# Layer 1's context keys and values woven into the latents' input projection, and stationary-only operands shifted by 64 bytes

## The reference, cut to what matters

```python
h = modulate(x, lp["g_norm1"], sh1, sc1)
hc = modulate(xc, lp["g_norm1"], modc[..., :d], modc[..., d:2 * d])
proj = h @ lp["w_in"]
n_in_c = IN_COLS if update_ctx else KV_COLS
projc = hc @ lp["w_in"][:, :n_in_c]
k_mla_l, v_mla_l, k_gqa_l, v_gqa_l = mixer_kv(proj[..., :KV_COLS], lp, rope_mla, rope_gqa)
k_mla_c, v_mla_c, k_gqa_c, v_gqa_c = mixer_kv(projc[..., :KV_COLS], lp, None, None)
...
def mixer_kv(kvc, lp, rope_mla, rope_gqa):
    c_kv, k_rope, k_g, v_g = jnp.split(kvc, ...)
    kv = (rms_norm(c_kv, lp["g_ckv"]) @ lp["w_ukv"]).reshape(b, l, MLA_HEADS, MLA_NOPE + MLA_V)
    ...
```

## Time and profile before

| | us |
|---|---|
| median of 3 runs | 2702.24 (2700.51 to 2708.99) |
| the profiled execution's own time | 2704.51 |
| its span in the trace | 2702.7 |
| PE busy in it | 2525.1 (93%) |
| PEld / DVE / ACT / POOL busy | 2216.8 / 1595.2 / 1326.6 / 582.2 |

### The profile page before, as it was taken

How to read it: one execution, slowest core, us unless ns; L and a number is a source line. 1 busy time by engine, 2 the same in 40 slices (tenths; PEclk the granted TensorE clock), 3 DMA queues, 4 the chain that set the end, 5 groups by cost and what they waited for, 6 DMA issues and landing times.

```text
span 2702.7 us, 46044 instructions
## 1 busy us (share of the span) xinstructions
PE 2525.1 (93%) x17246; PEld 2216.8 (82%) x17246; DVE 1595.2 (59%) x2386; ACT 1326.6 (49%) x2127; POOL 582.2 (22%) x430
## 2 busy tenths in 40 slices
PE   6999999999899996999999999997999899989997
PEld 5877898887689985875899799786898699758986
DVE  3655676567477755664777465435665544455445
ACT  3434565444547643445466445444544554455444
POOL 1111333210023322110233233020231232012311
PEclk8999999999999997999999999999999899999999
DMA  8575455546145553465556556562366466524663
GB/s 273 175 233 188 149 179 185 181 145 217 36 154 171 179 163 101 149 196 179 170 157 187 185 184 200 160 184 93 115 188 192 145 181 195 163 83 130 186 200 116
DMA packets 332944, 450.52 MB, mean 167 GB/s; under 512 B 28192, under 2 KB 207392, under 8 KB 332768
## 3 DMA queue, kind: packets, MB, share of 16 engines
q1 hardware_dynamic: 332400, 446.58, 52.8%
q0 software_dynamic: 368, 1.57, 0.2%
HBM read 446.99 MB, written 1.05 MB: 166 GB/s over the span
## 4 chain that ended last, share of the span: by engine, by line
PE 86%; DVE 7%; ACT 4%; issue 2%; DMA 1%; POOL 1%; SPq 1%; DVEq 0%; ACTq 0%; POOLq 0%
PE S L925 28%; PE S L916 23%; PE G L925 14%; PE G L916 9%; PE TB L978 2%; PE S L1007 2%; PE G L867 1%; PE G L1045 1%; ACT pp L1318 1%; DVE wlo L672 1%; ACT whi L666 1%; PE TB L891 1%; PE G L1030 1%; DVE nmx L1795 1%; PE S L1115 1%
## 5 line engine op out<-in xcount | busy, mean ns | idle before, releaser
L672 DVE TENSOR_TENSOR wlo<-raw,whi 128x1024 fp32r<-128x1024 f32 (+4 forms) x630 | 796.4, 1274 | 748.3 <-ACT whi L666 744.3
L666 ACT CAST whi<-raw 128x1024 fp32r<-128x1024 f32 (+2 forms) x776 | 771.7, 1008 | 754.0 <-PE S L916 280.8
L925 PE MATMUL S<-hhi,whi 128*128 128x256 f32 x1952 | 547.0, 280 | 4.1 <-issue 2.4
L925 PE MATMUL S<-hhi,wlo 128*128 128x256 f32 x1952 | 546.7, 280 | 0.0
L925 PE MATMUL S<-hlo,whi 128*128 128x256 f32 x1952 | 546.6, 280 | 0.0
L672 POOL TENSOR_TENSOR wlo<-raw,whi 128x1024 fp32r<-128x1024 f32 (+3 forms) x146 | 335.8, 2300 | 788.8 <-ACT whi L666 788.1
L925 PEld LDWEIGHTS S<-hhi,whi 128*128 128x128 f32 x1952 | 367.1, 188 | 5.7 <-issue 5.1
L925 PEld LDWEIGHTS S<-hlo,whi 128*128 128x128 f32 x1952 | 367.8, 188 | 0.1
L925 PEld LDWEIGHTS S<-hhi,wlo 128*128 128x128 f32 x1952 | 366.9, 188 | 0.0
L925 PE MATMUL G<-hhi,whi 128*128 128x256 f32 x1088 | 305.5, 281 | 1.9 <-issue 1.8
L925 PE MATMUL G<-hlo,whi 128*128 128x256 f32 x1088 | 304.8, 280 | 0.0
(11 more groups left out here) (336 smaller groups left out, 4227.9 us busy)
## 6 DMA issues: line engine op xcount, KB each, us to landing
raw<-in_ffn_wi SPq DMA_DIRECT2D x352, 256.0 KB, 3.5
raw<-in_w_up SPq DMA_DIRECT2D x264, 256.0 KB, 3.5
modw<-in_w_mod SPq DMA_DIRECT2D x192, 256.0 KB, 4.9
raw<-in_w_in SPq DMA_DIRECT2D x192, 256.0 KB, 3.0
raw<-in_ffn_wo SPq DMA_DIRECT2D x160, 256.0 KB, 3.5
raw<-in_w_down SPq DMA_DIRECT2D x120, 256.0 KB, 3.3
raw<-in_a_wqkv SPq DMA_DIRECT2D x72, 256.0 KB, 2.9
raw<-in_w_o SPq DMA_DIRECT2D x48, 256.0 KB, 3.3
```

Of the source, the lines that this page charges most:

```text
L666: act.copy(whi[:, n0 % SPLIT, z, w], raw[:, n0 % RAW, z, w]).then_inc(hi_done, 1)
L672: eng.tensor_tensor(wlo[:, n0 % SPLIT, z, w], raw[:, n0 % RAW, z, w], whi[:, n0 % SPLIT, z, w].bitcast(F32), ALU.subtract)\
L925: mm = pe.matmul(out_[:, m * T:(m + 1) * T], w, x, start=first and c == 0 and m == 0 and z == 0, stop=last and c == kc - 1 and z == len(te ...
```

## The change

It has two parts.

**The order in layer 1.** After the context's two `in` units the latents' `norm` comes at once. Its squares are taken by ACT after the context's first unit and its means by DVE after the second (`early`). Then the context's `prep` runs on DVE between the lo parts of the latents' first two `in` units (`part=0`), `ctrans` follows, the third unit (`part=1`), `gqat`, `ukv`, then the last two units (`part=2`) with the context's `heads` woven in, then `mlat`. The context's projected columns go to an unused place in `qkv1` (`rows_base`, `C_ASIDE`), and in these parts DVE makes every lo part (`lo_by_pool` returns False).

**Addresses.** Operands that only ever stand stationary are placed so that they start at a multiple of 128 bytes: `rhi` 125568 and `rlo` 117376 (new names over the same space as `hhi` and `hlo`, for `qkv`, `pgate` and `wo1`), `crT` 105088, `b_fhi` 174080 and 146176, `b_flo` 146176 and 168704, `b_phi` 154368. `hhi` and `hlo` of the `norm` stages and of the wide `norm2` ones, which are moving in `gates` and `up`, stay 64 past such a multiple, as do the attention outputs. To make room, the 8-column tensor `mx` is dropped and its users write to `ssq` or in place to `nmx`. The weights start at 72192 and 88576, still multiples of 128.

```diff
+SHIFT = 16
...
+            if l == DEPTH - 1:
+
+                add("prep", rq=2, rr=2, l=l, s=CTX, full=False)
+                gemm("in", 2, KD, l=l, s=s, splits=splits[:2], part=0)
+                add("ctrans", tk=1, sa=1, l=l, full=False)
+                gemm("in", 1, KD, l=l, s=s, splits=splits[2:3], part=1)
+                add("gqat", tk=1, s=CTX, full=False)
+                gemm("ukv", 2, 2, l=l, s=CTX)
+                add("heads", rq=2, rr=2, l=l, s=CTX, full=False)
+                gemm("in", 2, KD, l=l, s=s, splits=splits[3:], part=2)
+                add("mlat", tk=4, s=CTX, full=False)
...
-        sb("align_weights", [P, 24])
...
-        sb("align_operands", [P, 16])
+        sb("align_operands", [P, SHIFT])
...
+        ybuf, hlo, rlo, probT0 = region(KD * T + SHIFT, [("ybuf", 0, [P, NT, D], F32), ("hlo", 0, [P, KD, T], F32R),
+                                                         ("rlo", SHIFT, [P, KD, T], F32R), ("probT0", 0, [P, KD, T], F32)])
+        hhi, rhi, probT1 = region(KD * T + SHIFT, [("hhi", SHIFT, [P, KD, T], F32R), ("rhi", 0, [P, KD, T], F32R),
+                                                   ("probT1", 0, [P, KD, T], F32)])
...
-             ("b1_fhi", o1["gT"], [P, NF, T], F32R),
-             ("b1_flo", 0, [P, NF, T], F32R),
+             ("b1_fhi", o1["gT"] + SHIFT, [P, NF, T], F32R),
+             ("b1_flo", SHIFT, [P, NF, T], F32R),
...
+        def by_rows(st):
+            return (hhi, hlo) if st.wide else (rhi, rlo)
...
-            if st.kind in ("wo2", "gates") or st.kind == "down" and not st.conv or st.kind == "br" and st.part == 0:
+            if st.kind in ("wo2", "gates") or st.kind == "down" and not st.conv or st.part is not None and st.kind in ("br", "in") and (st.kind, st.part) != ("br", 1):
                 return False
...
+                        if k == 0 and early(st):
+                            act.wait_ge(bank_free[1], st.u + 1)
+                            for t in range(NT):
+                                row_squares(early(st), t)
...
+                    if st.part in (0, 2):
+                        work = prep_rows(before(st, "prep")) if st.part == 0 else head_rows(before(st, "heads"))
+
+                        def lo_and_rows(n0, *slot):
+                            lo_part(dve, n0, *slot)
+                            next(work, None)
```

More of the change, by code:

```diff
@@ L559, in inner, with early, rows_base @@
             return z if z and z.kind == "norm" else None
+        def early(st):
+            z = STAGES[STAGES.index(st) + 1] if st.kind == "in" else None
+            return z if z and z.kind == "norm" else None
+        def rows_base(st):
+            full = st.full if st.kind in ("prep", "ctrans", "heads") else st.s == LAT or st.l < DEPTH - 1
+            return 0 if full else C_ASIDE
         def inside(st):
@@ L1090, in _ @@
                                 tr.then_inc(turned_done, 1)
-                elif st.kind in ("in", "qkv", "pgate"):
+                elif st.kind == "in":
                     product(st, hhi, hlo, False)
+                elif st.kind in ("qkv", "pgate", "wo1"):
+                    product(st, rhi, rlo, False)
                 elif st.kind == "gates":
@@ L1096, in _ @@
                     pe.wait_ge(rows_ready, st.rr)
-                    srcs = [0, P] + ([C_CQ + c * P for c in range(Q_RANK // P)] if st.full else [])
+                    base = rows_base(st)
+                    srcs = [base, base + P] + ([C_CQ + c * P for c in range(Q_RANK // P)] if st.full else [])
                     for n in range(st.counts["tk"]):
@@ L1235, in _ @@
                 if st.kind == "norm" and not inside(st):
-                    if st.which == "1" and st is not norms[0]:
+                    if st.which == "1" and st is not norms[0] and not early(STAGES[STAGES.index(st) - 1]):
                         for t in range(NT):
@@ L1572, in prep_rows @@
                     k3 = q1[:, t, C_KG:C_VG].rearrange("p (h d) -> p h d", h=GQA_KV)
+                    if not st.full:
+                        rope_keys(st, t)
                     link(dve.tensor_copy(kdup1[:, t, :, 0], k3))
@@ L1673, in _ @@
                     if st is not norms[0]:
-                        for t in range(NT):
-                            row_mean(st, t)
+                        if not early(STAGES[STAGES.index(st) - 1]):
+                            for t in range(NT):
+                                row_mean(st, t)
                         for t in range(NT):
@@ L1717, in rows_in, with unit_and_rows @@
                         bank(st, 1, k)
-                        dve.tensor_copy(qkv1[:, 1, c0:c1], acc(st, j, 1)[:, 0:c1 - c0]).then_inc(bank_free[1], 1)
-                    units(st, rows_in)
-                elif st.kind == "prep":
-                    if not st.full:
-                        for _ in prep_rows(st):
-                            pass
+                        base = rows_base(st)
+                        dve.tensor_copy(qkv1[:, 1, base + c0:base + c1], acc(st, j, 1)[:, 0:c1 - c0]).then_inc(bank_free[1], 1)
+                        if k == 1 and early(st):
+                            for t in range(NT):
+                                row_mean(early(st), t)
+                    if st.part in (0, 2):
[3 more added lines that the diff above has]
+                            next(work, None)
+                        def unit_and_rows(k, j, i):
+                            split_weights(st, j, i, k, lo_and_rows)
+                            rows_in(k, j, i)
+                        over_units(dve, st, unit_and_rows)
+                        for _ in work:
+                            pass
+                    else:
+                        units(st, rows_in)
                 elif st.kind == "ukv":
@@ L1733, in _ @@
                     units(st, q_rows)
-                elif st.kind == "heads":
-                    if not st.full:
-                        for _ in head_rows(st):
-                            pass
                 elif st.kind == "gates":
```

69 lines of the change are left out of this document (38 added, 31 removed).

## The result

The changed kernel takes 2681.1 us (median of 4 runs, 2674.6 to 2681.6) against 2702.4 (2700.5 to 2709.0): a ratio of 0.991, 95% interval 0.9899 to 0.9922. That is 21.3 us less, 10 fewer than forecast, inside the range and on the side that had most of the chance. The profiled execution has a span of 2679.3 us, 23.4 under that of before.

What follows compares the result with a forecast made beforehand. PE, busy 93% of the span, was taken as the bound. The profiled 2704.5 us less 16.4 (order) and 14.5 (addresses) gave 2673.6, a median forecast of 2671; its own range 2655 to 2682, the wider range 2638 to 2704.

Steps and rivals of the forecast that it cites:

- Late squares: Context's last slot in layer 1: its cast waits behind ACT's squares of the latents' rows, costing PE about 1.0 us.
- The norm: Latents' norm in layer 1, from the context's last product to the latents' first: 2.4 plus 5.3, together 7.7 us.
- First two units and wait: Latents' first two `in` units: PE needs 11.8 us, DVE 16.7, so `ctrans` waits about 5.1 us.
- Transposes: Layer 1, four transposes for `ctrans` and four for `gqat`, 1.1 us each.
- `mlat`: Layer 1, after the last two units: 16 transposes with their copies, 4.0 us.
- Clock: Layer 1: gap before the norm and wait before `ctrans` can drop the granted clock; 1.5 us, bounds 0 and 4.6.
- side remark on POOL: Lo parts: with POOL out, DVE's prices may be a tenth lower, moving no term by over 1 us.
- the two placements of before: 256-column products at equal size: weights moving with activations stationary 0.1136 us, activations moving with weights stationary 0.1178 us.
- take 4.6 from the finer reading: Address part: 0.1180 against 0.1134 us taken as an address's worth, 4.6 ns on 3156 matmuls, 14.5 us saved.
- The controls: Spacings expected unchanged: `in` of layer 0 at 233 ns, and the products with weights stationary at 118.
- The spacing did not stay: Rival for the address part: excess belongs to the moving side, so spacing stays and only the order counts; 2686, chance 0.23.
- No collision: Rival for the address part: both operands on the same multiple collide; 2700 or 2715; chance 0.14 up to 5.2 ns, 0.08 beyond.

## Why the prediction was right or wrong

**The sum came close through terms that did not.** Forecast: 16.4 + 14.5 = 31. Measured in the two profiles: about 19 for the order, some 13 for spacing at full clock, 1.8 at the kernel's start, and 11 given back, 6.5 of them by the clock.

*Part one: right in mechanism, and 3 us too small.* The forecast was one wait of some 5 us before the transposes of `b_qkv`, none for the MLA heads, and 70 us from the context's last product to `gates`; it was 4.7, none and 65.8. By terms:
- Late squares: 1.0 forecast, 0.9 measured (the context's two units took 13.2 us instead of 12.3), but they lie ahead of the last product and so not in the 65.8, where I had counted them. That explains 1 of the 4 us between 70 and 65.8.
- The norm: 7.7 forecast, 5.8 measured. I took the 5.3 us from first turn to first product from the trace of before, from a stretch whose mean clock was 0.70. Here the clock was at 1.00 and it was 3.6.
- First two units and wait: 11.8 and 5.1; 12.0 and 4.7. (16.7 less 11.8 is 4.9; for the other 0.2 there is no row.)
- Transposes: 2.2; 1.1 and 0.4.
- `ukv`: 5.6 and 5.6. `mlat`: 4.0 and 3.3.
- Clock: 1.5, with bounds 0 and 4.6; 2.2, all of it in the 48 products after the wait.

The bounds of 9 to 23 us held the 19.1. My side remark on POOL misread a mean: of the six 512-wide lo parts one began while POOL was at its own and took 1390 ns, and the others took 679 to 693. That bears the remark out, and the sum, which had 0.7 for such a lo part, is not touched. The step that I left out was the load: I wrote that SP's queue loads the same slots in another order, and costed it at nothing. It was a link of the chain. DVE was nearly as late itself: it was busy for 11.27 of the 12.0 us of the first two units (the second stretch above).

*Part two: the reading was wrong, and its number near the measured one by luck.* I read the two placements of before as one operand's start in a stretch of 128 bytes. The step that failed is "take 4.6 from the finer reading": it compared a 256-column product with activations moving to one with weights moving, and took the difference for the price of an address. The `up` stage at 113.3 with the addresses of before shows that it is none: the 4.6 ns came off without any address moved. What moved the 512-column spacing is where one operand lies against the other in 256 bytes, with a second level at some distances that is not explained. By groups:
- 1848 products of `down`: 4.6 ns each forecast, 6.6 measured (distance 64 to 0).
- 1056 of `qkv`, `pgate` and `wo1`: 4.6 forecast, 0.9 measured (64 to 128).
- The other 252 (`crT`, `b_phi`): 4.6 forecast; `ukv`, with `crT` at distance 128, stood at 232.5 (5.58 / 24), so 0.8 there.
- `wo2`: nothing forecast, 4.2 measured, by the weights' move, which I noted as "still multiples of 128" and dropped.
- The controls: `in` of layer 0 at 233.3 and `up` at a mean of 117.9, both unchanged, as said. But the control proved nothing. `in`'s two operands went to 192 and 64, and what kept it at 233.3 is not shown: by the table, two passes of three at 229 would make 230.4. `up` kept its mean while its single spacings, mostly 117 to 119 before, spread to between 114 and 120. The last part of my forecast had the right warning ("distances other than 128 bytes matter: the weights moved by 128, `hlo` by 128 against `hhi`"), and I gave it no price.

*The rivals.* The spacing did not stay, so the argument that a cost which grows with the columns must be the moving side's is refuted too: with everything at distance 0, `qkv` lost 5.6 ns by a move of its stationary operand alone. No collision, as far as `down` goes. The Trainium skill (TensorE: Matmul & The Clock Gate, "Step-by-step: what each phase is for") says that loading the next tile's weights takes no read bandwidth from the running matmul; by it the stationary operand's place would not count. The trace does not bear that out for these products: the spacing of one and the same stream depends on where the stationary operand lies against the moving one (232.3 and 226.7 ns in `qkv`). By what mechanism is open.

*The chances.* The parts for "faster by over 0.3%" add to 0.775, and I wrote "some 0.76"; nothing hangs on it.

*What no step had.* The clock's return of the gain. I looked for it where the order changes and nowhere else. A `pgate` or `up` stage that follows a norm can start at 1.2 GHz, and whether it did changed in stages 500 us and more away from the changed order. The `pgate` stages started at full clock in both kernels with the addresses of before, which points at the addresses, but by one profile each that is not shown.

## What to carry to other kernels

When the addresses of large operands are chosen, count the distance between moving and stationary operand in 256 bytes, for each kind of product and number of columns by itself, and measure what it does as the length of a stage over its number of products; a shift of one tensor changes the distance of everything that is multiplied with it. A control that is to show "no change" must keep that distance, not only its own address. And where a chain on another engine is woven into PE's stream, give it one unit more than its busy time needs: the wait that is left costs its length and then, in the products behind it, half as much again by the clock (4.7 and 2.2 us here).

## What the runs showed of the hardware

- The spacing of fp32r products at the full clock depends on the distance of the two operands modulo 256 bytes, by up to 6.6 ns in 233.4 (3%), the table above. The best distance for 512 columns with the activations stationary (0: 226.7) is the worst for 256 columns with the weights stationary (119.9), and 256 columns with the activations stationary are slow there too (119.6, against 113.6 at 64).
- At some placements there are two levels: for 256 columns with the weights stationary 113.3 and 117.8 ns at distance 192, 117.3 and 118.7 at 160; for 512 columns with the activations stationary 228.9 and 233.3 at 192, 232.4 and 233.3 at 128. A level mostly holds for a whole stage, changes where a new stage begins or, in a few places, at the end of a unit of 96 products, and differs between two executions of the same program. From an `up` to the `down` that follows it without a gap it was carried over (eight of eight at 192). What decides it is open.
- After the same 3.8 us wait and the same 16 transposes, a `pgate` stage began with 3 to 4 us at a granted clock of 0.50 to 0.56 in some kernels and at 1.00 in others: the clock had fallen in both and came back earlier in the latter.
